# Chunk 0 of a depthwise convolution: from TensorE to ACT and POOL, issued between other work

## What is computed

```python
def hybrid_mixer(h, w_in, conv_dw, conv_b, ...):
    u = h @ w_in
    a_val, a_gate, b_gate, c_gate, b_x, p_in, gate_logits = jnp.split(u, _SPLITS, axis=-1)
    a = a_val * jax.nn.sigmoid(a_gate)
    a = causal_depthwise_conv(a, conv_dw) + conv_b      # 512 channels, width 31
    a = jax.nn.silu(layer_norm(a, conv_ln_g, conv_ln_b))
    y_a = a @ w_pa
    s = causal_depthwise_conv(c_gate * b_x, short_dw)   # 256 channels, width 3
    y_b = (b_gate * s) @ w_pb
    p = ...                                             # trailing means of p_in, per-group map
    y_c = p @ w_pc
    g = jax.nn.sigmoid(gate_logits).reshape(bsz, seq, N_BRANCH, D_MODEL)
    merged = g[..., 0, :] * y_a + g[..., 1, :] * y_b + g[..., 2, :] * y_c
    return merged @ w_o
```

## Time and profile before

| | us |
|---|---|
| median of 2 runs | 6164.78 (6164.72 to 6164.84) |
| profiled execution | 6162.59 |
| its span on the slowest core | 6160.8 |
| TensorE busy in it | 5941.7 (96%) |
| VectorE (DVE) busy | 2102.8 (34%) |
| ScalarE (ACT) busy | 1304.0 (21%) |
| GpSimd (POOL) busy | 522.7 (8%) |
| matmuls of L575 (wide convolution) | 473.5 |

### The profile page before, as it was taken

One profiled execution on the slowest core, in us unless ns is written; L12 is line 12 of the kernel. 1 busy time (PEld: TensorE's weight loads), 2 busy tenths in 40 slices (PEclk: granted clock), 3 DMA queues, 4 the chain that ended last, 5 costly groups with the idle time before them and its releaser, 6 DMA issues.

```text
span 6160.8 us, 61620 instructions; the slowest of 8 cores (6151.4 to 6160.8 us)
## 1 busy us (share of the span) xinstructions
PE 5941.7 (96%) x26149; PEld 2847.8 (46%) x26656; DVE 2102.8 (34%) x3074; ACT 1304.0 (21%) x2105; POOL 522.7 (8%) x812
## 2 busy tenths in 40 slices
PE   7999999999999999999999999999999999999999
PEld 3454444544445444454444544445444454444544
DVE  1244223442334422343223442234322333224332
ACT  1122111221212211222122221122212222112221
POOL 0010000100001000010000100001000010001000
PEclk9999999999999999999999999999999999999999
DMA  4424435244552444524455244442445424353243
GB/s 94 71 49 74 78 62 89 42 73 71 113 85 43 72 75 68 84 44 72 79 101 88 42 75 69 79 79 42 75 89 96 83 41 75 63 92 66 48 69 79
DMA packets 129201, 444.67 MB, mean 72 GB/s; under 512 B 12960, under 2 KB 13216, under 8 KB 128928
## 3 DMA queue, kind: packets, MB, share of 16 engines
q0 software_dynamic: 111744, 406.90, 39.5%
q1 hardware_dynamic: 17184, 33.81, 1.9%
HBM read 830.73 MB, written 16.78 MB: 138 GB/s over the span
## 4 chain that ended last, share of the span: by engine, by line
PE 93%; ACT 3%; DVE 2%; DMA 1%; issue 1%; SPq 0%; DVEq 0%; ACTq 0%
PE ps L479 20%; PE ps L473 19%; PE ps L502 19%; PE ps L812 11%; PE ps L575 7%; PE ps L519 7%; PE ps L857 4%; PE ps L829 3%; PE ps L415 2%; DMA x<-xT 1%; DVE h L428 1%; ACT sq L412 1%; ACT a_act L629 1%; PE ps L598 0%; PE ps L594 0%
## 5 line engine op out<-in xcount | busy, mean ns | idle before, releaser
L473 PE MATMUL ps<-h,ring 128*128 128x512 bf16 x5512 | 1343.3, 382 | 30.7 <-DVE h L428 21.3
L479 PE MATMUL ps<-h,ring 128*128 128x512 bf16 x5516 | 1329.2, 381 | 6.2
L502 PE MATMUL ps<-R,ring 128*128 128x512 bf16 x5521 | 1217.7, 379 | 5.8
L487 DVE TENSOR_TENSOR R<-R,ps 128x512 bf16<-128x512 f32 x704 | 483.2, 688 | 1885.9 <-PE ps L479 1873.4
L484 ACT ACTIVATE R<-ps 128x512 f32<-128x512 f32 x704 | 420.5, 597 | 2599.2 <-PE ps L473 2599.0
L473 PEld LDWEIGHTS ps<-h,ring 128*128 128x128 bf16 x5632 | 550.8, 98 | 712.9 <-DVE h L428 55.3
L479 PEld LDWEIGHTS ps<-h,ring 128*128 128x128 bf16 x5632 | 553.6, 98 | 670.9 <-issue 13.0
L382 POOL DMA_DIRECT2D ring<-wstream x776 | 413.6, 538 | 5240.3 <-PE ps L473 1930.3
L502 PEld LDWEIGHTS ps<-R,ring 128*128 128x128 bf16 x5632 | 549.9, 98 | 663.0 <-issue 1.8
L812 PE MATMUL ps<-h,ring 128*128 128x512 bf16 x3008 | 677.8, 383 | 4.9 <-issue 2.0
L507 DVE SCALAR_TENSOR_TENSOR x<-ps,x 128x512 f32<-128x512 f32 x512 | 351.1, 691 | 755.1 <-PE ps L502 755.1
(11 more groups left out here) (72 smaller groups left out, 2001.1 us busy)
## 6 DMA issues: line engine op xcount, KB each, us to landing
ring<-wstream POOLq DMA_DIRECT2D x776, 512.0 KB, 6.2
x<-xT SPq DMA_DIRECT2D x8, 2048.0 KB, 26.5
yT<-a_act SPq DMA_DIRECT2D x8, 1024.0 KB, 4.5
yT<-sbb SPq DMA_DIRECT2D x8, 512.0 KB, 5.9
yT<-pp SPq DMA_DIRECT2D x8, 512.0 KB, 6.4
params_sb<-params SPq DMA_DIRECT2D x1, 172.0 KB, 2.8
consts_sb<-consts SPq DMA_DIRECT2D x1, 80.0 KB, 2.5
```

Of the source, the lines that this page charges most:

```text
L473: S.op("pe", lambda e, bg=bg, slot=slot, kc=kc, tt=tt: e.matmul(ps[:, bg, :], ring[:, slot, kc * 128:(kc + 1) * 128], h[:, kc, tt * TT:(tt ...
L479: S.op("pe", lambda e, bu=bu, slot=slot, kc=kc, tt=tt: e.matmul(ps[:, bu, :], ring[:, slot, 1024 + kc * 128:1024 + (kc + 1) * 128], h[:, k ...
L487: S.op("dve", lambda e, bu=bu, k=k, fi=fi, tt=tt: e.tensor_tensor(out=act_v[:, fi, tt * TT:(tt + 1) * TT], in0=sg_v[:, k, :], in1=ps[:, bu ...
L502: S.op("pe", lambda e, b=b, ws_=ws_, off=off, fi=fi, tt=tt, n=len(fs): e.matmul(ps[:, b, :], ring[:, ws_, off:off + 128], act_v[:, fi, tt ...
```

## The change

Chunk 0 no longer goes through `conv`. For each half its 31 taps become a chain: ACT writes `acc = w0 * a` and, for each further tap, a product into one of two buffers `cprod`; POOL adds it into `acc`; at the end ACT writes `co` with the bias. These 64 items (per half one start, 30 pairs, one end) are put on a list, `backlog`, and taken off it a few at a time between other work: three at each `release_unit` (behind the transfer on POOL's queue), two at places between the helpers, two after every third tap of a `conv` on TensorE, and what is left after `conv(3)`. `av(0)` becomes the first unit of the mixer, `av(1)` comes before the pool sums, and `c_pool(1)` after `diag_build(2)`. `acc` lies in the upper part of R3, which gets a region name of its own, R3b, where the FFN and the merge (`mg`) also use it.

```diff
-W_IN_ORDER = [10, 12, 8, 11, 13, 9, 14, 15, 4, 0, 5, 1, 6, 2, 7, 3]
+W_IN_ORDER = [4, 0, 10, 12, 8, 11, 13, 9, 14, 15, 5, 1, 6, 2, 7, 3]
...
+        cprod = sb("cprod", [128, 2, TT], F32)
...
+        acc_v = R3[:, 6144:7168].rearrange("p (r t) -> p r t", r=NT)
+        OFFPE_CONV = (0,)
+        backlog = []
...
+        def drain_backlog(n):
+            for _ in range(min(n, len(backlog))):
+                backlog.pop(0)()
+
         def release_unit():
             issue_unit()
+            drain_backlog(3)
...
             def diag_build(j):
+                if j in OFFPE_CONV:
+                    return
...
+            def conv_offpe(j):
+                RACC = [("R3b", "acc")]
+                for tt in range(NT):
+                    ra = [("a", j, tt)] + ([("a_halo", j)] if tt == 0 else [("a", j, tt - 1)])
+                    for k in range(CW):
+                        wk = params[:, pb + P_CW + j * CW + k: pb + P_CW + j * CW + k + 1]
+                        src = a_v[:, j, tt * TT + k:tt * TT + k + TT]
+                        if k == 0:
+                            backlog.append(lambda tt=tt, wk=wk, src=src, ra=ra: S.op("act", lambda e: e.activation(
+                                out=acc_v[:, tt, :], in_=src, func=AF.Copy, scale=wk),
+                                reads=ra + ["params"], writes=[("acc", tt)], regions=RA + RACC))
+                        else:
+                            def pair(tt=tt, wk=wk, src=src, ra=ra):
+                                r = rot("cprod", 2)
+                                S.op("act", lambda e: e.activation(
+                                    out=cprod[:, r, :], in_=src, func=AF.Copy, scale=wk),
+                                    reads=ra + ["params"], writes=[("cprod", r)], regions=RA)
+                                S.op("pool", lambda e: e.tensor_tensor(
+                                    out=acc_v[:, tt, :], in0=acc_v[:, tt, :], in1=cprod[:, r, :], op=ALU.add),
+                                    reads=[("acc", tt), ("cprod", r)], writes=[("acc", tt)], regions=RACC)
+                            backlog.append(pair)
+                    backlog.append(lambda tt=tt: S.op("act", lambda e: e.activation(
+                        out=co_v[:, j, tt * TT:(tt + 1) * TT].bitcast(F32R), in_=acc_v[:, tt, :], func=AF.Identity,
+                        bias=params[:, pb + P_CB + j:pb + P_CB + j + 1], scale=0.5),
+                        reads=[("acc", tt), "params"], writes=[("co", j, tt)], regions=RCO + RACC))
+
             def conv(j):
+                if j in OFFPE_CONV:
+                    return
...
+                    if k % 3 == 2:
+                        drain_backlog(2)
...
+            av(0)
+            if 0 in OFFPE_CONV:
+                conv_offpe(0)
+                drain_backlog(2)
+            else:
+                diag_build(0)
             s0 = next_unit("win")
             b_cgate(0, s0, 0)
+            drain_backlog(2)
             b_bx(0, s0, 1)
             release_unit()
...
             c_pin(0, s3, 0)
+            drain_backlog(2)
             c_pin(1, s3, 1)
             release_unit()
-            diag_build(0)
-            av(0)
+            diag_build(1)
+            av(1)
+            if 0 not in OFFPE_CONV:
+                conv(0)
             c_pool(0)
-            av(1)
-            conv(0)
-            diag_build(1)
-            c_pool(1)
+            drain_backlog(2)
             av(2)
             conv(1)
             diag_build(2)
+            c_pool(1)
             av(3)
             conv(2)
             diag_build(3)
...
             conv(3)
+            drain_backlog(len(backlog))
```

More of the change, by code:

```diff
@@ L355, in stage_chunk @@
                     return buf[:, c - c0, :].bitcast(F32), [(nm, c - c0, t_) for t_ in range(NT)]
+        acc_v = R3[:, 6144:7168].rearrange("p (r t) -> p r t", r=NT)
+        OFFPE_CONV = (0,)
+        backlog = []
         ident_v = consts[:, 0:128]
         corr_v = consts[:, 128:160].rearrange("p (c t) -> p c t", c=2)
-        state = {"bank": 0, "sq": 0, "sg": 0, "tg": 0, "tga": 0}
+        state = {"bank": 0, "sq": 0, "sg": 0, "tg": 0, "tga": 0, "cprod": 0}
         def new_bank():
@@ L485, in ffn @@
                             out=sg_v[:, k, :], in_=ps[:, bg, :], func=AF.Silu),
-                            reads=[("ps", bg)], writes=[("sg", k)], regions=[("R3", "ffn")])
+                            reads=[("ps", bg)], writes=[("sg", k)], regions=[("R3", "ffn"), ("R3b", "ffn")])
                         S.op("dve", lambda e, bu=bu, k=k, fi=fi, tt=tt: e.tensor_tensor(
@@ L489, in ffn @@
                             op=ALU.mult),
-                            reads=[("ps", bu), ("sg", k)], writes=[("act", fi, tt)], regions=[("R3", "ffn")])
+                            reads=[("ps", bu), ("sg", k)], writes=[("act", fi, tt)], regions=[("R3", "ffn"), ("R3b", "ffn")])
                     if rel:
@@ L799, in mixer @@
             RP = [("R3", "P2")]
-            RM = RP
+            RM = [("R3", "P2"), ("R3b", "P2")]
             RT = RP
@@ L844, in mixer @@
                         op=ALU.add),
-                        reads=[("tg", 0, r), ("tg", 2, r)], writes=[("mg", j, tt)], regions=RP)
+                        reads=[("tg", 0, r), ("tg", 2, r)], writes=[("mg", j, tt)], regions=RM)
                 release_unit()
```

## The result

The changed kernel is **slower by 2.1%**: ratio to the kernel before 1.0208, 95% interval 1.0194 to 1.0222. Its profiled execution took 6295.3 us (span 6293.4 on the slowest core, the others down to 6284.6); the one of before took 6162.6. Against the forecast of 6240 that is another 55 us, inside the range. The interval reaches just under 2%, so a loss of more than 2% is likely but not certain. In many executions, of the kernel before too, the cores of one die show a lower granted clock and the time is longer; executions without this are compared. All eight cores show a mean granted clock of 0.967 to 0.969, where it was 0.986 to 0.988.

The account below looks back on a forecast made before the run. TensorE, busy 96% of the span, bounds the kernel; conv(0) and order save 16.5 us a mixer, but waits and slow matmuls make it 127.1 against 117.7: +9.4, eight mixers +75, so 6240 us, range 6060 to 6340.

Parts of the forecast that it names:

- the sharing: POOL and DVE operations with two SBUF inputs holding each other up: 20.3 us a mixer before diag_build(2), 1.9 after.
- wait in conv(2): TensorE waits 19.4 us a mixer in the middle of conv(2), at k = 16, for POOL's half of diag_build(2).
- wait in conv(3): TensorE waits a second time, 2.8 us a mixer, before conv(3)'s second half, for POOL's half of diag_build(3).
- The price of an add: Each 512-column add on POOL takes 1.15 us start to start, including about 0.05 for waiting on its predecessor.
- The lower bound (0.98): Cheapest add on POOL: 0.98 us for 512 elements, from L560's 1.72 ns an element.
- the bound with a dearer second stream: Dearest add on POOL: 1.42 us, if a true second stream costs half as much again as L560's repeated operands.
- the sum made from it (27.7, 6284): If each operation fully blocks the other side, sharing takes its bound of 27.7 us a mixer and the time is 6284.
- The clock: After the wait in conv(2), some 12 matmuls run at half rate, 2.3 us; conv(3)'s second half takes 7.2.
- the order: av(0) first puts eight more matmuls inside the wait for h at the mixer's start: 1.7 us a mixer, 13.8 in all.
- B: Rival, chance 0.15: POOL and DVE hardly hinder each other, no wait in conv(2), 2.3 us in conv(3); 6062 us.
- C: Rival, chance 0.2: an add on POOL costs more than 1.15 us; 6308 us at 1.30, 6363 at 1.42.
- D: Rival, chance 0.15: DVE falls behind in the bgates, TensorE waits for PSUM in av(1), some 3 us a mixer; 6308 us.

Follow-up runs that it names:

- the first three versions with the shared chunk: Against the kernel before, all of chunk 0 off TensorE, half 0 on ACT and POOL, half 1 on DVE: profiled 6132.0, 6151.8 and 6084.5 us.

## Why the prediction was right, and by what it was off

The mechanism and its places were right: POOL late from the first units on, no TensorE wait before conv(2), a long one in the middle of conv(2) ended by POOL's diag_build, a short one at the same place in conv(3), ACT late without TensorE caring (it starts the two tanh of av(2) at 357.5, whose matmuls had ended by 347.0). The size was near in part by luck: up to diag_build(2) the adds were taken 11.3 us too cheap and the sharing some 10 us too dear. The change was forecast as +75 us and came out as +128. In numbers, from the first matmul of the mixer:

| term | forecast | measured, first mixer |
|---|---|---|
| conv(1) begins | 50.4 | 50.2 |
| conv(2) reaches its upper half | 79.7 | 79.4 |
| diag_build(2) ready | 99.1 | 104.7 |
| wait in conv(2) | 19.4 | 25.3 |
| diag_build(3) ready | 119.9 | 128.5 |
| wait in conv(3) | 2.8 | 5.8 |
| conv(3) ends | 127.1 | 138.2 |

**The price of an add** was the largest error: 1.41 us start to start against the 1.15 taken. 44 adds cost 61.9 us instead of 50.6. The lower bound (0.98) had rested on L560's 1.72 ns an element with 0.10 fixed; with two full operands POOL needs 2.1 ns and 0.18. The step that failed is the scaling by DVE's ratio, which kept L560's repeated operands in the price; the bound with a dearer second stream, 1.42, was nearly the truth. The Trainium skill (GPSIMD Engine Reference, section 3.1) gives 2.6 cycles an element for two inputs, an estimate of 1.11 us at 1.2 GHz for 512 before what is fixed; with the 0.18 of these runs that is 1.29, against 1.26 measured. The prediction divided the section's 2048-element time by four, and so kept only a quarter of the fixed part. The wait on the add before was 0.19 us (the run with the chains in turn), not 0.05.

**The sharing** was put at nearly twice what it cost, and hid a part of this. Of 84.7 us from POOL's transfer at 312.97 (the gate that the prediction had at 15.8) to the start of diag_build(2) at 397.70, adds take 61.9, the diag half 3.4, transfers 3.5, and hand-overs between ACT and POOL 5.3 (2.2 were allowed). That leaves 10.6 for sharing, where 20.3 stood. Added up row by row (each group of adds against 1.41 a step, the first diag half against 3.40) it is about 12, as the remainder counts a gap behind the last add of every group. Its sign and its places were right, and the run without the pool sums shows it as a cause. The rule of the Trainium skill (SBUF — State Buffer, "Who interferes with whom"), that an operation in progress shuts out the other side in full, agrees with the rows in both directions, DVE's 2.2 us and POOL's 2.08; the sum made from it (27.7, 6284) lands near the result only because the add was priced too low.

**The sum of these** leads to diag_build(2): 99.1 + 11.3 - 9.7 + 3.1 + 0.3 (transfers) + 0.5 (start) = 104.6, against 104.7 measured. It closes because sharing is what was left over; what it shows is the size of each term.

**The clock.** Conv(3)'s second half was put at full speed after a short wait; it took 9.8 us, 2.6 more, with a granted clock of 0.50 from 425 to 430. Conv(2)'s was foreseen (2.3). And the order gained 3.3 us a mixer, not 1.7, because the first mixer was the one in which the kernel before had no slow stretch after the wait for h. Taking one mixer as the pattern hid that the other seven took 1.4 us longer.

**Rivals.** B (no sharing, 6062) falls by the run without the pool sums. C (dearer adds; 1.42 gives 6363) had the add right and the sharing of the forecast with it, and so came out 70 us too high. D (TensorE waits for PSUM before conv(1)) did not happen in the changed kernel: DVE's L713 were stretched to 1.67 us, and still every bank was free in time. Its idea, DVE late in its own queue, is what held back the first three versions with the shared chunk.

## What to carry to other kernels

Work handed to an idle engine is paid at that engine's price, and in its queue: add up the whole queue, transfers and builds included, and see what stands behind the new work, also on the engine that feeds it (here ACT's PSUM copies), before counting what the busy engine is rid of. The half that fits (30 adds a mixer) gained 1.5%, some 0.4% of it by the order alone; the whole (60) lost 2.1%. Two engines that hinder each other are best given their work at different times; the lowest times of four kernels with the same work in other places lay between 6035 and 6114 us. Not tried was the whole load with POOL's diag_build named ahead of the adds in its own queue.

## What the runs showed of the hardware

- POOL's fp32 add of two full operands: 0.25 us for 32 columns, 1.26 for 512; repeated operands are cheaper (3.40 for 1920). A wait on the add before it costs 0.19 us.
- DVE operations with two SBUF inputs and POOL's adds took turns, each waiting out the other (2.08 instead of 1.26 us for the add, 2.2 instead of 1.23 for the sum); a DVE operation costs POOL its own length less some 0.4 to 0.7 us, so those of 0.75 us cost it 0.27.
- After 7 us in which TensorE did only sixteen matmuls, the granted clock was 0.55 for 3.4 us in seven of eight mixers; with 24 matmuls in the same 7 us it stayed at 1.00 in all eight, in the run with the order alone. Filling a wait can be worth more than the matmuls that fill it.
